# Weight units carried in pairs: a ring of four places of 2 MB where there were eight of 1 MB

## The reference

```python
m_lat = (jax.nn.silu(c) @ w_mod + b_mod)[:, None, :]        # per layer, 1024 x 6144
...
pl = split_columns(u_lat @ w_in)                            # 1024 x 5888
...
merged = gates[..., :D_MODEL] * (branches[0] @ w_branch[0])
for i in range(1, N_BRANCH):
    merged = merged + gates[..., i * D_MODEL:(i + 1) * D_MODEL] * (branches[i] @ w_branch[i])
return merged @ w_out
...
a = jnp.einsum("becd,edf->becf", xs, w_gate)                # 16 experts, each 3 x 1024 x 1024
u = jnp.einsum("becd,edf->becf", xs, w_up)
y = jnp.einsum("becf,efd->becd", jax.nn.silu(a) * u, w_down) * sel_w[..., None].astype(h.dtype)
```

## Time and profile before

| | |
|---|---|
| runs | 3216.86, 3220.76, 3226.86 us, median 3220.76 |
| profiled execution | 3217.62 us, span 3215.8 |
| mean granted clock of PE | 0.952 |
| PE busy | 2790.3 us, 87% |
| DVE, ACT busy | 857.6 us, 343.2 us |
| moved by DMA | 676.19 MB, mean 210 GB/s |
| ring<-units | 624 transfers of 1024 KB, median 10.1 us from issue to landing |

### The profile page before, as it was taken

The page is one execution under the profiler, slowest core; times in us unless marked ns, Lnnn a source line. Parts: engine busy times, 40 slices in busy tenths (PEclk is TensorE's granted clock), DMA queues, the critical chain, the costliest instruction groups (busy, mean ns, idle before and its releaser), DMA issues.

```text
span 3215.8 us, 39515 instructions
## 1 busy us (share of the span) xinstructions
PE 2790.3 (87%) x16456; PEld 2008.8 (62%) x16456; DVE 857.6 (27%) x1758; ACT 343.2 (11%) x697; POOL 39.7 (1%) x70
## 2 busy tenths in 40 slices
PE   7999999978888879999555565699999999999998
PEld 3644454455655646888333233487888887888887
DVE  1322231242221234331211111389322102212200
ACT  0021120020000011220100000101210001111000
POOL 1000000000000001000000000000000000000000
PEclk9999999989999999999787878899999999999999
DMA  8434225149989973233599999743333443333441
GB/s 316 169 137 154 95 108 193 66 175 420 398 372 421 406 319 98 93 101 128 243 401 408 372 403 402 296 155 118 105 118 118 151 150 118 106 130 118 141 147 40
DMA packets 95644, 676.19 MB, mean 210 GB/s; under 512 B 11136, under 2 KB 12288, under 8 KB 15232
## 3 DMA queue, kind: packets, MB, share of 16 engines
q1 hardware_dynamic: 91488, 660.17, 52.4%
q0 software_dynamic: 4000, 13.64, 1.5%
HBM read 672.71 MB, written 1.05 MB: 210 GB/s over the span
## 4 chain that ended last, share of the span: by engine, by line
PE 74%; DMA 18%; DVE 3%; issue 2%; SPq 1%; ACT 1%; ACTq 0%; DVEq 0%
PE ps L566 28%; DMA ring<-units 18%; PE ps L827 10%; PE ps L947 10%; PE ps L852 2%; PE ps L1200 2%; PE ps L1005 2%; PE ps L1036 2%; PE ps L584 2%; PE ps L575 1%; PE ps L655 1%; PE ps L651 1%; PE ps L981 1%; SPq L474 1%; PE ps L776 1%
## 5 line engine op out<-in xcount | busy, mean ns | idle before, releaser
L947 PE MATMUL ps<-ring,arena 128*64 128x256 f32 (+1 forms) x6144 | 602.4, 441 | 259.7 <-DMA ring<-units 236.4
L947 PEld LDWEIGHTS ps<-ring,arena 128*64 128x64 f32 (+1 forms) x6144 | 374.6, 140 | 471.4 <-issue 346.0
L566 PE MATMUL ps<-h,ring 128*128 128x256 f32 (+1 forms) x2240 | 518.1, 393 | 4.9 <-ACT h L1359 4.9
L566 PEld LDWEIGHTS ps<-h,ring 128*128 128x128 f32 x2240 | 426.7, 191 | 94.0 <-issue 37.8
L827 PE MATMUL ps<-u,ring 128*128 128x512 f32 (+1 forms) x1024 | 339.5, 487 | 6.5 <-DMA ring<-units 6.5
L566 PE MATMUL ps<-arena,ring 128*128 128x256 f32 x1408 | 306.6, 379 | 4.7 <-DVE arena L2115 3.4
L566 PEld LDWEIGHTS ps<-arena,ring 128*128 128x128 f32 x1408 | 267.3, 190 | 42.1 <-DVE arena L2115 4.2
L827 PEld LDWEIGHTS ps<-u,ring 128*128 128x128 f32 x1024 | 193.6, 190 | 141.3 <-issue 119.6
L2011 DVE COPY u<-ps 32x512 f32<-32x512 f32 (+1 forms) x128 | 70.8, 553 | 310.7 <-PE ps L947 309.4
L2158 DVE SCALAR_TENSOR_TENSOR arena<-arena,vec 128x256 f32<-128x256 f32 x240 | 97.1, 481 | 0.0
L566 PE MATMUL ps<-u,ring 128*128 128x512 f32 (+1 forms) x256 | 87.8, 504 | 10.6 <-DVE u L1687 10.6
(11 more groups left out here) (313 smaller groups left out, 2446.6 us busy)
## 6 DMA issues: line engine op xcount, KB each, us to landing
ring<-units SPq DMA_DIRECT2D x624, 1024.0 KB, 10.1
arena<-quarters POOLq DMA_DIRECT2D x32, 256.0 KB, 2.9
h<-tokens SPq DMA_DIRECT2D x1, 2048.0 KB, 25.9
arena<-neighbours POOLq DMA_DIRECT2D x32, 64.0 KB, 3.9
arena<-tokens POOLq DMA_DIRECT2D x1, 2048.0 KB, 8.7
con<-constants SPq DMA_DIRECT2D x1, 1712.0 KB, 21.1
h<-memory POOLq DMA_DIRECT2D x1, 1024.0 KB, 6.0
out<-h SPq DMA_DIRECT2D x2, 512.0 KB, 3.2
```

What stands on the lines that cost most here:

```text
L566: last = nc.tensor.matmul(ps[:, g + j, 0:n], w[:, kt, j * P:(j + 1) * P], rhs[:, q * KT + kt, 0:n], start=(q == 0 and kt == 0), stop=(q == ...
L947: last = nc.tensor.matmul(ps[j * slots:(j + 1) * slots, bank, lo:lo + UC], lhsT[:, kt, 0:slots], w[j][:, kt, :], start=(kt == 0), stop=(kt ...
```

## The change

Two consecutive units become one row of the array `units`: partition by partition, unit 2k and then unit 2k + 1, 16 KB on each. `ring` has four places of two units. SP issues 312 transfers of 2 MB; the one that brings units 2k + 8 and 2k + 9 waits until `units_used` is at least 2k + 2. There are four semaphores in place of eight, and `unit()` waits for the one of the pair that holds its unit. What PE computes and the points at which it adds to `units_used` stay as they are. The constants' second part is loaded after unit 11, where it was after unit 10. SBUF for the ring is of the same size.

```diff
--- before.py
+++ after.py
@@ -25,6 +25,7 @@
 UNIT = 2048
 UC = UNIT // KT
 RING = 8
+PAIRS = RING // 2
 DEPTH = 2
 HD = 64
 E = 16
@@ -148,7 +149,8 @@
         early = [xa[l]["k"][1:]] if l else [xa[l]["v"][:1]]
         parts += early + [xa[l]["q"], xa[l]["v"][0 if l else 1:], xa[l]["o"]]
         parts += [units_of(i["mlp_w1_2"][l]), units_of(i["mlp_w2_2"][l])]
-    return np.concatenate(parts, 0)
+    stream = np.concatenate(parts, 0)
+    return stream.reshape(-1, 2, P, UNIT).transpose(0, 2, 1, 3).reshape(-1, P, 2 * UNIT)
 
 
 def branch_quarters(w):
@@ -248,7 +250,7 @@
 
 def build(nc, ap, out):
     units = ap["units"]
-    n_units = units.shape[0]
+    n_units = 2 * units.shape[0]
     with ExitStack() as ctx:
         def sb(name, *shape):
             return ctx.enter_context(nc.sbuf_tensor(name, [P, *shape], F32))
@@ -257,7 +259,7 @@
             return ctx.enter_context(nc.semaphore(name))
 
 
-        ring = sb("ring", RING, UNIT)
+        ring = sb("ring", PAIRS, 2 * UNIT)
         vec = sb("vec", NVEC)
         con = sb("con", NCON)
         h = sb("h", KT, 2 * S)
@@ -390,7 +392,7 @@
         constants_loaded = sem("constants_loaded")
         bias_loaded = sem("bias_loaded")
         memory_loaded = sem("memory_loaded")
-        loaded = [sem(f"unit_loaded_{s}") for s in range(RING)]
+        loaded = [sem(f"unit_pair_loaded_{s}") for s in range(PAIRS)]
         units_used = sem("units_used")
         products_taken = sem("products_taken")
         dve_step, act_step = sem("dve_step"), sem("act_step")
@@ -456,22 +458,20 @@
             sp.dma_start(vec[:, :], ap["vectors"]).then_inc(vectors_loaded, 16)
             sp.dma_start(con[:, 0:P + 2], ap["constants"][:, 0:P + 2]).then_inc(vectors_loaded, 16)
 
-            for s in range(RING):
+            for s in range(PAIRS):
                 sp.dma_start(ring[:, s, :], units[s]).then_inc(loaded[s], 16)
             sp.dma_start(h[:, :, :], ap["tokens"]).then_inc(inputs_loaded, 16)
-            for s in range(3):
-                sp.wait_ge(units_used, s + 1)
-                sp.dma_start(ring[:, s, :], units[RING + s]).then_inc(loaded[s], 16)
-            sp.dma_start(con[:, P + 2:], ap["constants"][:, P + 2:]).then_inc(constants_loaded, 16)
-            for s in range(3, RING):
-                sp.wait_ge(units_used, s + 1)
-                sp.dma_start(ring[:, s, :], units[RING + s]).then_inc(loaded[s], 16)
+            for s in range(PAIRS):
+                sp.wait_ge(units_used, 2 * s + 2)
+                sp.dma_start(ring[:, s, :], units[PAIRS + s]).then_inc(loaded[s], 16)
+                if s == 1:
+                    sp.dma_start(con[:, P + 2:], ap["constants"][:, P + 2:]).then_inc(constants_loaded, 16)
             turns = n_units // RING - 1
             assert n_units % RING == 0
             with sp.Fori(0, turns - 1) as i:
-                for s in range(RING):
-                    sp.wait_ge(units_used, i * RING + RING + s + 1)
-                    sp.dma_start(ring[:, s, :], units[bass.ds(i * RING + 2 * RING + s, 1)]
+                for s in range(PAIRS):
+                    sp.wait_ge(units_used, i * RING + RING + 2 * s + 2)
+                    sp.dma_start(ring[:, s, :], units[bass.ds(i * PAIRS + RING + s, 1)]
                                  .rearrange("a p n -> (a p) n")).then_inc(loaded[s], 16)
             norms = 5 * DEPTH + 1
             for lo, hi in ((0, 4), (4, KT)):
@@ -522,14 +522,15 @@
                 n = state["unit"]
                 pe_wait_unit(n)
                 state["unit"] += 1
-                return ring[:, n % RING, :].rearrange("p (k c) -> p k c", c=UC)
+                at = n % 2 * UNIT
+                return ring[:, n % RING // 2, at:at + UNIT].rearrange("p (k c) -> p k c", c=UC)
 
             def pe_wait_unit(n):
                 value = 16 * (n // RING + 1)
                 if count.turn is None:
-                    pe.wait_ge(loaded[n % RING], value)
+                    pe.wait_ge(loaded[n % RING // 2], value)
                 else:
-                    pe.wait_ge(loaded[n % RING], count.turn * (16 * state["body"] // RING) + value)
+                    pe.wait_ge(loaded[n % RING // 2], count.turn * (16 * state["body"] // RING) + value)
 
             def loop(times, body, per):
```

## The result

The changed kernel takes 3273.72 us (median of 3270.46 to 3283.92), against 3221.95 for the kernel before beside it: 1.0166 times as long, interval 1.0138 to 1.0195. The forecast was 3277. The profiled execution took 3270.46 with a span of 3268.6, 52.8 us more than that of before.

What follows compares the result with a forecast made beforehand. Transfers were taken to bound the two expert stages and PE the rest. The terms, 30.4 + 12.5 + 19.9 + 2.5 - 6 = +59.3 us on 3217.62, gave 3276.9, stated as 3277, range 3245 to 3300.

Steps and rivals of the forecast that it cites:

- the parity: Layer 0's bursts and experts (unit 75) begin at odd units and straddle pairs; layer 1's experts (unit 294) don't.
- Term 1: Five modulation bursts (L632, L801): the second half's transfer is issued only after the first half; +30.4 us.
- Term 2: Behind the stalls in the five bursts PE's clock drops, 2.5 us five times; +12.5 us.
- Term 3: Layer 0's expert stage: queued units lost at the ends of four groups, 4.98 us each; +19.9 us.
- Term 4: Start, project(u): unit 8 comes with unit 9, 2.49 us later; +2.5 us.
- Term 5: Transfers awaited in both expert stages: fewer, with 16 KB runs, taken as 0.7% faster; -6 us.
- the one in which a transfer pays for itself in a full queue: Rival: each transfer costs fixed engine time even in a full queue, so merging is faster; 3195 at 0.5 us; chance 0.04.
- Term 6: Layer 1's expert chunks take two whole pairs and keep their spacing; later blocks hide transfers; 0 us.

Runs made afterwards that it cites:

- aligned_pairs: Changed kernel with one empty ring place before units 8 and 267, so bursts and expert stages begin on whole pairs; 3238.41 us.
- pairs_in_experts: Kernel before with aligned 2 MB pairs in the two expert stages only, single units elsewhere; 3207.22 us, 0.9963 of the kernel before.
- odd twin: pairs_in_experts without its two empty ring positions, so layer 0's expert chunks straddle two pairs; 3227.22 us, 1.0025 of the kernel before.
- pairs_in_8k_runs: Changed kernel with units stored as before, each 2 MB transfer reading two 8 KB runs per partition; 3291.80 us, 1.0231 of the kernel before.
- second profile: The changed kernel, unchanged, run and profiled once more; median 3280.63 us, 1.0195 of the kernel before.
- both_by_pair: Kernel before, still 1 MB transfers, but SP issues and PE waits by pair; 3288.64 us, 1.0213 of the kernel before.

## Why the prediction was right, point by point

**What binds, and the parity.** Shown. Odd starts cost, even ones don't, in the bursts (aligned_pairs) and in the experts (pairs_in_experts against its odd twin).

**Term 1, the late transfer, 30.4.** The mechanism is shown. The term is the growth of the waits, and these are 40.1 us where 8.1 stood: 32.0, so 1.6 too small. The gaps are 7.8 to 8.2 us, not 7.5: the pair is there 7.6 us after its issue, where a unit's 4.74 and 2.49 more would make 7.23. None of it was absorbed.

**Term 2, the clock, 12.5.** Real. What the bursts grew by beyond the waits is 11.4 us (43.4 less 32.0), of which the second halves have 10.2; filling the gaps wins back 8.4 net in the bursts, and what it wins in the whole time is not settled. The term was a little too large and term 1 a little too small, so that their sum, 42.9 against 43.4, is nearer than either.

**Term 3, the lookahead, 19.9.** Shown at its size with small transfers, 10.3 and 10.0 for each half and 19.3 for both. The twins in the experts differ by 17.5. In the changed kernel the stage is longer by 10.7 and 14.2 with the faster stream in it; an estimate of that gain from 427 against 421 GB/s is 1.4% of the 418 us in which units are awaited, 5.9, which leaves 16.6 and 20.1 for the term. The two profiles also differ in the granted clock (the third group has 1.00 in the first and 0.97 in the second), but that this makes the difference is not shown.

**Term 4, the start, 2.5.** Measured 1.4 and 1.7: the first matmul of project(u) starts at 36.25, not 34.80. The direction held; why it is a microsecond less stays open.

**Term 5, the stream, -6.** The sign is right and the reason (16 KB runs, not fewer transfers) fits, with the reservation above; the size is too small: 427 against 421 GB/s is 1.4%, twice the 0.7% taken. Of the rivals, the one in which a transfer pays for itself in a full queue is out: pairs_in_8k_runs has half as many transfers and is slower. The Trainium skill, in "DMA: Bandwidth & Descriptors", section Bandwidth, gives 341 GB/s at 1 MB and 425 at 16 MB, for transfers issued from GpSimd; these here are issued from SP. The prediction's estimate from the fit of that page of the Trainium skill, 6.8 us for one transfer of 2 MB against 8.8 for two of 1 MB, would have made the expert stages a fifth shorter; in the filled queue no run here shows it.

**Term 6, layer 1, 0.** Held in the changed kernel within what a profile can tell (-1.7 and -0.3). But 1.4% of the 458 us of term 5 would be 6.5 us less, and neither this nor any other kernel shows so much there (pairs_in_experts has -4.0). That, and the longer stage of the three kernels with small transfers by pair, is not explained.

**The sum.** +59.3 was forecast and the profiled execution shows +52.8. The bursts are within 0.5 us, partly by the luck of two errors that cancel; most of the difference, 6.2 us, is layer 0's expert stage in the first profile (10.7 for 16.9). In the second profile, +60.9 in the total, that stage has 14.2.

## What to carry to other kernels

Before transfers are merged, find the places where the reader takes several pieces at once, and count whether these places begin on a piece of the merged size. A merged piece arrives at its last byte and frees its place at its last use; where a burst straddles it, a transfer that ran beside the first half of the burst is issued behind it. In a stage bound by transfers, look at the stretches in which the reader frees nothing: the ring has to cover them, and each half piece that is held or awaited comes off the ring.

## What the runs showed of the hardware

In a full queue halving the number of transfers gained nothing by itself: 1 MB in 8 KB runs moved 420 to 421 GB/s (before and both_by_pair), 2 MB in 8 KB runs from two blocks 415 (pairs_in_8k_runs), 2 MB in 16 KB runs from one block 427 (changed and pairs_in_experts). I had not expected the middle one to be the slowest.

Behind gaps of 7.8 to 8.2 us the 64 matmuls of a half took 5.5 to 6.1 us at a granted clock of 0.59 to 0.66; with the gaps filled by other matmuls all second halves took 3.66 us (the first of them at 1.00).
